# Split float32 products whose moving columns go in 64-byte pieces from both halves in turn, with two buffers moved by 64 bytes

## The reference

```python
def _swiglu(h, w_gate, w_up, w_down):
    return (jax.nn.silu(h @ w_gate) * (h @ w_up)) @ w_down
...
    for i in range(DEPTH):
        x = x + 0.5 * _swiglu(_rmsnorm(x, ffn1_norm[i]), ffn1_w_gate[i], ffn1_w_up[i], ffn1_w_down[i])
        proj = _rmsnorm(x, mix_norm[i]) @ w_in[i]
```

## Time and profile before

| | |
|---|---|
| median of 3 runs | 2014.86 us |
| the profiled execution, its own time | 2016.84 us |
| its span in the trace | 2014.9 us |
| granted TensorE clock | 1.00 of full speed throughout |
| TensorE busy, matmuls | 1978.3 us, 15795 instructions |
| TensorE busy, weight loads | 1820.1 us |
| GpSimd busy | 1493.5 us |
| ScalarE, VectorE busy | 1038.7 us, 945.3 us |
| DMA | 329 MB, 163 GB/s on the mean |

### The profile page before, as it was taken

How to read it: one execution, slowest core, us unless ns; L and a number is a source line. 1 busy time by engine, 2 the same in 40 slices (tenths; PEclk the granted TensorE clock), 3 DMA queues, 4 the chain that set the end, 5 groups by cost and what they waited for, 6 DMA issues and landing times.

```text
span 2014.9 us, 37053 instructions
## 1 busy us (share of the span) xinstructions
PE 1978.3 (98%) x15795; PEld 1820.1 (90%) x15795; DVE 945.3 (47%) x1589; ACT 1038.7 (52%) x1551; POOL 1493.5 (74%) x652
## 2 busy tenths in 40 slices
PE   7999999999999999999999999999999999999998
PEld 7998788989989998788899989999999899999997
DVE  3550766434205550776343304745576028356750
ACT  5444456464436444456464547455644374656442
POOL 6789454459887789446368887768789977687896
PEclk9999999999999999999999999999999999999999
DMA  6756332136555656333135565545555655455553
GB/s 222 243 178 209 105 126 92 41 123 197 186 202 176 217 184 204 94 105 106 44 127 189 188 236 160 168 147 183 173 178 197 198 159 163 147 193 170 179 200 126
DMA packets 250965, 329.10 MB, mean 163 GB/s; under 512 B 9008, under 2 KB 225586, under 8 KB 250418
## 3 DMA queue, kind: packets, MB, share of 16 engines
q1 hardware_dynamic: 250802, 326.73, 49.6%
HBM read 325.66 MB, written 1.05 MB: 162 GB/s over the span
## 4 chain that ended last, share of the span: by engine, by line
PE 60%; DVE 3%; issue 1%; ACT 1%; POOL 0%; DVEq 0%; ACTq 0%
PE psA L410 12%; PE psA L411 12%; PE psA L412 12%; PE psB L410 5%; PE psB L412 5%; PE psB L411 5%; PE psB L1939 1%; PE psA L1781 1%; DVE hT_lo L1168 1%; PE psA L2111 0%; PE psA L2113 0%; PE psA L1782 0%; PE psA L1787 0%; DVE small L1522 0%; PE psB L2101 0%
## 5 line engine op out<-in xcount | busy, mean ns | idle before, releaser
L1022 POOL TENSOR_TENSOR w_lo<-raw,w_hi 128x1024 fp32r<-128x1024 f32 x600 | 1457.9, 2448 | 501.0 <-ACT w_hi L597 500.1
L410 PE MATMUL psA<-xT_hi,w_lo 128*128 128x256 f32 x3168 | 897.5, 283 | 6.2 <-POOL w_lo L1022 4.1
L411 PE MATMUL psA<-xT_lo,w_hi 128*128 128x256 f32 x3168 | 884.7, 279 | 0.0
L412 PE MATMUL psA<-xT_hi,w_hi 128*128 128x256 f32 x3168 | 883.8, 279 | 0.0
L597 ACT ACTIVATE w_hi<-raw 128x1024 fp32r<-128x1024 f32 x600 | 630.4, 1052 | 362.7 <-PE psB L412 237.5
L410 PEld LDWEIGHTS psA<-xT_hi,w_lo 128*128 128x128 f32 x3168 | 594.9, 188 | 17.5 <-issue 11.8
L411 PEld LDWEIGHTS psA<-xT_lo,w_hi 128*128 128x128 f32 x3168 | 594.4, 188 | 3.4 <-issue 3.3
L412 PEld LDWEIGHTS psA<-xT_hi,w_hi 128*128 128x128 f32 x3168 | 594.0, 187 | 0.0
L1168 DVE TENSOR_TENSOR hT_lo<-hfull,hT_hi 128x256 fp32r<-128x256 f32 x132 | 219.9, 1698 | 2.1 <-ACT hT_hi L730 0.8
L410 PE MATMUL psB<-w_hi,hT_lo 128*128 128x512 f32 x528 | 205.6, 389 | 0.4 <-issue 0.4
L412 PE MATMUL psB<-w_hi,hT_hi 128*128 128x512 f32 x528 | 205.5, 389 | 0.0
(11 more groups left out here) (440 smaller groups left out, 2303.8 us busy)
## 6 DMA issues: line engine op xcount, KB each, us to landing
raw<-in_w_in SPq DMA_DIRECT2D x78, 1024.0 KB, 5.1
raw<-in_ffn_w_gate SPq DMA_DIRECT2D x44, 1024.0 KB, 5.2
raw<-in_ffn_w_up SPq DMA_DIRECT2D x44, 1024.0 KB, 5.2
raw<-in_ffn_w_down SPq DMA_DIRECT2D x44, 1024.0 KB, 4.9
raw<-in_w_ffn_in SPq DMA_DIRECT2D x44, 1024.0 KB, 4.9
raw<-in_w_ffn_out SPq DMA_DIRECT2D x22, 1024.0 KB, 4.8
raw<-in_w_out SPq DMA_DIRECT2D x16, 1024.0 KB, 4.8
raw<-in_w_branch_da SPq DMA_DIRECT2D x4, 1024.0 KB, 4.9
```

Source lines behind the costliest of these rows:

```text
L410: nc.tensor.matmul(o, a_lo, b_hi, start=start, stop=False, skip_group_check=skip)
L411: nc.tensor.matmul(o, a_hi, b_lo, start=False, stop=False, skip_group_check=skip)
L412: return nc.tensor.matmul(o, a_hi, b_hi, start=False, stop=stop, skip_group_check=skip)
L1022: nc.gpsimd.tensor_tensor(split_half(w_lo, n, kind), raw_half(n, kind), split_half(w_hi, n, kind).bitcast(F32), ALU.subtract)\
```

## The change

`product` and `project_entry` give TensorE the same matmuls in the same order, with another order of columns inside each: the moving operand and the PSUM output are seen as two halves of pieces of 16 columns (64 bytes), and the pieces are taken in turn from the first and the second half. For 256 columns that is piece 0, 8, 1, 9 and so on to 7, 15; for 512 columns 0, 16, 1, 17; for the 2 x 128 operand of `project_two` the two halves are the two slots. Each column lands where it did. Two unused tensors of 64 bytes replace the one: the first is ahead of the arena, the second behind it, so that modulo 512 the arena is at 64 and xT at 128, with the weights' slots at 0 as before. The instructions of VectorE, ScalarE, GpSimd and SyncE, their shapes and their waits, are the same; those of TensorE stand in the same order.

```diff
+LINE = 16
...
         x = sb("x", [P, RB, D])
+        sb("lines1", [P, 16])
         ARENA = 107 * KB
         slab = sb("slab", [P, ARENA // 4])
         at0 = nc.sbuf_base - ARENA
-        sb("line", [P, 16])
+        sb("lines2", [P, 16])
         xT_hi = sb("xT_hi", [P, KC, L], F32R)
...
+        def step(v):
+
+            if len(v.shape) == 3:
+                return v.rearrange("p h (j n) -> p j h n", n=LINE)
+            return v.rearrange("p (h j n) -> p j h n", h=2, n=LINE)
+
         def product(o, a_hi, a_lo, b_hi, b_lo, start, stop, skip=False):
 
+            o, b_hi, b_lo = step(o), step(b_hi), step(b_lo)
             nc.tensor.matmul(o, a_lo, b_hi, start=start, stop=False, skip_group_check=skip)
...
-                        M(psA[:, t, 0:L], split_half(w_lo, s + t, "A")[:, kc, :], xT_hi[:, kc, :], start=(kc == 0), stop=False)
+                        M(step(psA[:, t, 0:L]), split_half(w_lo, s + t, "A")[:, kc, :], step(xT_hi[:, kc, :]), start=(kc == 0), stop=False)
```

More of the change, by code:

```diff
@@ L1780, in project_entry @@
                     for t in range(2):
-                        M(psA[:, t, 0:L], split_half(w_lo, s + t, "A")[:, kc, :], xT_hi[:, kc, :], start=(kc == 0), stop=False)
-                        M(psA[:, t, 0:L], split_half(w_hi, s + t, "A")[:, kc, :], xT_hi[:, kc, :], start=False, stop=False)
+                        M(step(psA[:, t, 0:L]), split_half(w_lo, s + t, "A")[:, kc, :], step(xT_hi[:, kc, :]), start=(kc == 0), stop=False)
+                        M(step(psA[:, t, 0:L]), split_half(w_hi, s + t, "A")[:, kc, :], step(xT_hi[:, kc, :]), start=False, stop=False)
                 for kc in range(KC):
@@ L1786, in project_entry @@
                     for t in range(2):
-                        ins_ = M(psA[:, t, 0:L], split_half(w_hi, s + t, "A")[:, kc, :], xT_lo[:, kc, :], start=False, stop=(kc == KC - 1))
+                        ins_ = M(step(psA[:, t, 0:L]), split_half(w_hi, s + t, "A")[:, kc, :], step(xT_lo[:, kc, :]),
+                                 start=False, stop=(kc == KC - 1))
                         if kc == KC - 1:
```

## The result

| | before | after |
|---|---|---|
| median | 2014.37 us (4 runs, 2012.49 to 2015.28) | 2061.99 us (4 runs, 2061.56 to 2062.57) |
| ratio, 95% interval | 1 | 1.0238 (1.022 to 1.0256) |
| span of the profiled execution | 2014.9 us | 2060.5 us |
| TensorE busy | 1978.3 us | 2029.2 us |
| TensorE's waits for GpSimd | 4.1 us | 0.6 us |

The prediction was 1960 us, between 1903 and 2018, with a chance of 0.73 of being faster. It is wrong in sign. The nearest of its cases was the slow rival, at 2045 us.

A forecast was written before the change was run, and what follows sets the result against it. TensorE's stream of matmuls was taken to bound the kernel. Shorter intervals sum to 58.1 us, less some 3 us lost to waits, so 55 us: median about 1960 us, range 1903 to 2018.

The forecast's parts named there:

- slow rival: Operand and PSUM access: each change of piece costs one column's time, 30 us more, 2045 us; chance 0.17.
- What bounds the kernel: Whole kernel: TensorE's stream of matmuls sets the end, busy in 98% of the span, waits under 30 us of 2014.9.
- two readers meet: TensorE's matmuls: moving stream and next weight load stop each other in one bank; without meetings 58.1 us less.
- the banks repeat every 512 bytes: Operand memory: the assumption that puts pieces 0 and 8, 512 bytes apart, in one bank; the 58.1 us rest on it.
- no variation with the k block: Matmul intervals: they stay the same while k-block addresses step by 512 and 1024 bytes, offered as support for the 512-byte repeat.
- lockstep: Moving stream and weight load: taken in turns, both advance one bank in 32 clocks, stay one or two banks apart, never meet.
- I take nothing: Runs of 16 columns in operands and PSUM results: 15 breaks in 256 columns cost 0, bounds nothing to 6.3 ns.
- The places: Arena and xT moved to 64 and 128 modulo 512: keeps the readers apart; the arena's move otherwise nothing, within 2 us.
- 16 clocks fixed: Every matmul form: 16 clocks remain without meetings, giving 113.3 ns for 256 columns and 220.0 ns for 512.
- the PSUM side: PSUM results: the slow case's breaks could cost on the write; shares its one column's time per break and 0.17 chance.
- Given back in waits: Mixer waits and the GpSimd waits after them: some 3 us of the gain lost (0 to 8).

The follow-up runs named there:

- micro1: Kernel of TensorE alone, 56 groups of float32r matmuls varying operand place and column order; 256 straight columns 113.3 to 120.0 ns, turns of 16 120.0 ns.
- micro3: Kernel of TensorE alone, 41 groups of 36 matmuls testing run distances and what ran before; 113.3 to 121.5 ns for runs of 16 columns.
- micro2: Kernel of TensorE alone, 43 groups of 48 matmuls, mostly 16 columns standing; turns of 8, 16, 32, 64 took 123.4, 120.0, 119.0, 113.3 ns.
- same_place: The changed kernel's column order, but arena and xT both at 0 modulo 512; 2061.0 us.
- psum_only: The changed kernel with only the PSUM output in turns, the moving operand straight on; 2037.5 us.
- places_only: The kernel before, columns straight on, with only the buffers moved to the change's places; 2039.0 us, ratio 1.0116.
- xt192: The kernel before, columns straight on, with the unused tensor ahead of xT 192 bytes instead of 64; 2006.12 us, ratio 0.9957.
- line8: The changed kernel with pieces of 8 columns (32 bytes) instead of 16; 2097.2 us.

## Why the prediction was wrong

- **What bounds the kernel**: right. TensorE's stream set the end in all kernels; when its matmuls got 50.9 us longer the span grew by 45.6, and the waits of the earlier trace rows shrank.
- **That the intervals come from where the operands lie, and that two readers meet**: the places right for the straight order, the meeting not shown. micro1 gives before's 120.0, 117.8, 226.7 and 233.3 ns with TensorE alone, and 256 columns have 113.3 ns once hardly any weight load runs beside them; but 512 columns then have 231.3 ns, more than the 226.7 with the full load at place 0, which a stop at each meeting doesn't give. The rule of the Trainium skill, TensorE: Matmul & The Clock Gate, Part 2, that the load takes nothing from the running matmul, would have made the gain 0. The runs speak against it for float32r: 226.7 against 233.4 ns with nothing changed but the place of the standing operand (L79 and L80).
- **"if the banks repeat every 512 bytes"**: the repeat that the runs show is 256. The check that the prediction offered, no variation with the k block, can't tell 256 from 512, since all steps there are multiples of both. The lockstep built on it needed that pieces 0 and 8 share a place, which holds for 256 too; the next point is what broke the forecast.
- **The failed step: "I take nothing" for the pieces.** Its support was project_two, one break of 4096 bytes, after which the place modulo 256 goes on as in a straight stream; by micro3 fifteen of that kind can be free. Eight of after's fifteen stay at a place, and that kind no row of before contained. Measured where hardly a load runs beside: 120.0 ns instead of 113.3 for 256 columns (micro1, L119 against L115), 240.0 instead of 231.3 for 512 (micro2). These 6.7 ns are more than the 4.44 that the forecast wanted to win. In the kernel all forms are at these values at any place, so nothing is won from the places either: 47 us slower instead of 55 faster. Why a stay at a place costs stays open.
- **The places**: the prediction gave them only the gain of never meeting, and priced no move by the values its own rows had for it. Measured alone, with straight columns, they cost 24 us. Under the order in turns they made no difference (same_place 2061.0 us, after 2062.0).
- **16 clocks fixed**: no kernel went below 113.3 ns for 256 columns; 220 ns for 512 columns was never seen in a steady stretch.
- **The slow rival** had the right sign and place (the read side was one of its two) and nearly the price: 119.6 and 232.9 ns against 120.0 and 240.0, 2045 against 2062 us. That the price was so near for 256 columns is luck: its law, one column's time for each break, added to 113.3, would give 126.2 ns for pieces of 8 and 116.2 for pieces of 32, where micro2 has 123.4 and 119.0. Its other half, the PSUM side, with the rule of the Trainium skill, PSUM — Partial Sum Buffer, Specifications, that any non-contiguous pattern slows matmuls significantly, fell: pieces of 64 bytes are free there (psum_only against places_only). Its 0.17 was too little, since the one thing that had no row was also the thing done in 12,000 matmuls.
- **Given back in waits**: foretold were 3 us of longer waits for 58 us of gain; measured are 5 us of shorter waits for 52 us of loss. The size is right, and the direction follows the sign.

What stays open: why pieces that stay at a place cost; why in turns of 16 the place against the weight load no longer counts; the value of 231 ns for 512 columns with 16 standing; and what leads to which of the two speeds. The last is worth the most: all of xT's matmuls at 113.3 ns in xt192 would be 25 us more (9888 x 2.6 ns), before what waits give back.

## What to carry to other kernels

Price a new access order by a small kernel that runs only it: three such kernels of under 0.5 ms told more here than the whole trace. When a change has two parts, an order and a move of buffers, give each its own line in the sum, and test each without the other as well as both: here the move alone cost 24 us, and nothing once the order was there. And where one form shows two steady speeds at one address, don't take the value of a single stretch for that of the address.

## What the runs showed of the hardware

- At full granted clock a float32r matmul of 256 columns had 113.3 ns where consecutive 64-byte pieces go on through the four places of a 256-byte window in turn (micro1, micro3; 116.7 to 117.8 in three groups of the same kind), 120.0 with two pieces at each place, 123.4 with four half pieces at each, 121.5 with all pieces at one place, all with 16 columns standing.
- The standing operand's place against the moving one, modulo 256 bytes, goes with 120.0 (0), 117.8 or 113.3 (64), 118.7 or 119.9 (128), 113.3 or 117.8 (192) for 256 straight columns, and with 226.7, 233.4, 232.4, 228.8 ns for 512 straight columns (standing operand at those places, micro1).
- One stream can run for many microseconds at either of two speeds, 113.3 or 117.8 ns, at one place; which one it was differed with the matmuls ahead of it (micro3).
- Writing a PSUM result in pieces of 64 bytes cost nothing (psum_only 118.7 and 233.3 ns, as places_only), and in pieces of 32 bytes nothing that shows (line8 123.3 and 243.3 ns, as with a straight result in micro2).
